# Two early experts instead of the last two hold their gate and up weights outside the ring, and token rows are stored once

## What is computed

```python
x = x + jnp.concatenate([att, lru_out], axis=-1) @ w_out[l]
h2 = rmsnorm(x, ffn_norm[l]).reshape(b * s, d)
# 4 groups of 8 experts; top 1 group, top 2 experts in it; combine = their weights
for g in range(N_GROUPS):
    hg = jax.nn.silu(jnp.einsum('nd,edf->nef', t, w_gate[g])) * jnp.einsum('nd,edf->nef', t, w_up[g])
    y = y + jnp.einsum('nef,efd->nd', hg * combine[:, g, :, None], w_down[g])
x = x + y.reshape(b, s, d)
return rmsnorm(x, final_norm)
```

## Time and profile before

| | us |
|---|---|
| median of 3 runs | 2077.38 |
| lowest, highest | 2074.16, 2081.77 |
| span of the profiled execution | 2074.0 |
| PE busy in it | 1971.6 (95%) |
| third mixture, first to last product of an expert | 1800.7 to 2050.1 |

### The profile page before, as it was taken

The page is one execution under the profiler, slowest core; times in us unless marked ns, Lnnn a source line. Parts: engine busy times, 40 slices in busy tenths (PEclk is TensorE's granted clock), DMA queues, the critical chain, the costliest instruction groups (busy, mean ns, idle before and its releaser), DMA issues.

```text
span 2074.0 us, 25525 instructions
## 1 busy us (share of the span) xinstructions
PE 1971.6 (95%) x10045; PEld 1050.5 (51%) x10045; DVE 691.6 (33%) x1669; ACT 404.9 (20%) x874; POOL 151.7 (7%) x205
## 2 busy tenths in 40 slices
PE   8999889999999999999999999999799999999887
PEld 4444446554545453746554545454554445765443
DVE  0155657311111112635321111112738233632214
ACT  1133433111111111112111111111223322122212
POOL 0111101000000000000100000000010001211100
PEclk9999999999999999999999999999999999999999
DMA  9711104999999999823899999999941111799995
GB/s 334 215 46 47 45 24 166 414 419 420 420 421 420 421 420 378 314 64 102 332 419 420 421 421 420 421 420 417 340 118 41 41 41 33 262 380 419 420 419 216
DMA packets 127026, 596.87 MB, mean 288 GB/s; under 512 B 17489, under 2 KB 46049, under 8 KB 64095
## 3 DMA queue, kind: packets, MB, share of 16 engines
q1 hardware_dynamic: 111567, 568.06, 68.9%
q0 software_dynamic: 15376, 27.68, 4.0%
HBM read 573.48 MB, written 37.01 MB: 294 GB/s over the span
## 4 chain that ended last, share of the span: by engine, by line
PE 81%; DMA 13%; DVE 3%; ACT 2%; issue 1%; SPq 0%; DVEq 0%; ACTq 0%
PE bank L1021 22%; PE bank L679 10%; PE bank L1063 10%; PE bank L930 10%; DMA ring<-in_w_up_dram 7%; DMA ring<-in_moe_w_up_dram 6%; PE bank L826 5%; PE bank L693 4%; PE bank L665 3%; PE bank L1194 1%; PE bank L778 1%; PE bank L755 1%; PE bank L1155 1%; PE bank L921 1%; PE bank L742 1%; PE bank L712 1%
## 5 line engine op out<-in xcount | busy, mean ns | idle before, releaser
L1021 PE MATMUL bank<-ring,work 128*64 128x512 f32 (+1 forms) x2976 | 559.0, 527 | 28.0 <-DMA ring<-in_w_up_dram 24.2
L1021 PEld LDWEIGHTS bank<-ring,work 128*64 128x64 f32 x2976 | 222.7, 138 | 360.2 <-issue 335.5
L1063 PE MATMUL bank<-ring,work 128*64 128x512 f32 x1280 | 295.8, 600 | 3.9 <-DVE work L1894 3.9
L1894 DVE COPY work<-bank 128x256 f32<-128x256 f32 (+1 forms) x96 | 36.5, 380 | 693.8 <-PE bank L922 693.8
L930 PE MATMUL bank<-work 128*128 128x128 f32 x2048 | 245.7, 278 | 0.0
L930 PEld LDWEIGHTS bank<-work 128*128 128x128 f32 x2048 | 233.5, 192 | 6.1 <-issue 2.0
L679 PE MATMUL bank<-hT,ring 128*128 128x512 f32 x512 | 234.2, 599 | 0.7 <-ACT work L1257 0.7
L1353 ACT ACTIVATE work<-bank 64x512 f32<-64x512 f32 x96 | 56.7, 590 | 540.8 <-PE bank L1063 540.8
L1063 PEld LDWEIGHTS bank<-ring,work 128*64 128x64 f32 x1280 | 84.2, 136 | 144.0 <-issue 129.1
L679 PEld LDWEIGHTS bank<-hT,ring 128*128 128x128 f32 x512 | 92.4, 191 | 104.6 <-issue 102.6
L1341 ACT ACTIVATE work<-bank 64x512 f32<-64x512 f32 (+1 forms) x96 | 49.8, 518 | 476.2 <-PE bank L1021 476.2
(11 more groups left out here) (314 smaller groups left out, 1717.8 us busy)
## 6 DMA issues: line engine op xcount, KB each, us to landing
ring<-in_moe_w_down_dram SPq DMA_DIRECT2D x128, 1024.0 KB, 16.3
ring<-in_moe_w_gate_dram SPq DMA_DIRECT2D x126, 1024.0 KB, 15.3
ring<-in_moe_w_up_dram SPq DMA_DIRECT2D x126, 1024.0 KB, 17.3
ring<-in_w_down_dram SPq DMA_DIRECT2D x32, 1024.0 KB, 26.3
ring<-in_w_gate_dram SPq DMA_DIRECT2D x30, 1024.0 KB, 22.1
ring<-in_w_up_dram SPq DMA_DIRECT2D x30, 1024.0 KB, 24.4
ring<-in_attn_w_qkv_dram SPq DMA_DIRECT2D x12, 1024.0 KB, 12.8
work<-y_rows SPq DMA_DIRECT2D x12, 1024.0 KB, 7.0
```

The lines of the kernel that those rows point to most:

```text
L1021: mm = pe.matmul(GU2[s % 2][BLK * a:BLK * a + BLK, 0:F], xgT[pair % 2][:, per * kk + k, BLK * of_pair:BLK * of_pair + BLK], v[a][k], start ...
L1063: mm = pe.matmul(DN[BLK * n:BLK * n + BLK, :], hT_[:, 2 * kk + k, :], v[:, k, 512 * n:512 * n + 512], start=(kk + k == 0), stop=(2 * kk + ...
```

## The change

- The pairs that stay outside the ring in the third mixture are those of experts 2 and 3 counted from 0 (the third and fourth). `load_spare` (expert 2, to `hT`) and `load_scraps` (expert 3, to `work` and the scraps) are called after SP's `slot` 3 instead of after `slot` 2. The scraps have a semaphore of their own. Experts 30 and 31 take their gate and up through the ring. The helpers count the experts of `spare_of` up to a slot instead of counting from the end.
- `x_rows` has 512 rows instead of 1024 and POOL stores each token row once. DVE adds one instruction that halves the row numbers into `x_row`, by which the rows are fetched; POOL's wait for row numbers (`slots_known`) comes after it.
- POOL's load of the final norm's gain waits for two uses of the pairs outside the ring (`spare_used`) instead of one.
- In the second block's mixer the semaphores `par.conv` and `par.forget` become one: DVE, ACT and PE each wait for all ten small loads.

```diff
-        spare_of = [range(E - n, E) for n in (1, 1, 2)]
+        spare_of = [(E - 1,), (E - 1,), (2, 3)]
...
         def spare_slot(m, i, s):
-            return spares_to(m, i, s) > 0
+            return type(i) is int and TURN * i + s in spare_of[m.l]
         def spares_to(m, i, s):
-            return max(0, TURN * i + s - E + 1 + len(spare_of[m.l])) if type(i) is int else 0
+            return sum(x <= (TURN * i + s if type(i) is int else TURN) for x in spare_of[m.l])
         def gu_unit(m, i, s):
-            return 0 if type(i) is int and TURN * i + s == 0 else m.upb * s - m.nd - SPARE * max(0, spares_to(m, i, s) - 1)
+            return 0 if type(i) is int and TURN * i + s == 0 else m.upb * s - m.nd - SPARE * (spares_to(m, i, s) - spare_slot(m, i, s))
...
-                    sources = expert_units(m, l, E - 1)
+                    sources = expert_units(m, l, spare_of[l][0])
...
-                    gate, up, _ = list(expert_units(m, l, E - 2))
+                    gate, up, _ = list(expert_units(m, l, spare_of[l][1]))
...
-                    if l == 2 and type(i) is int and j == 2:
+                    if l == 2 and type(i) is int and j == 3:
                         load_spare()
                         load_scraps()
...
+                    if l == 2:
+                        link(ins)
+                        ins = dve.tensor_scalar(x_row[:, :], y_row[:, :], 1, None, ALU.logical_shift_right)
                     ins.then_inc(slots_known, 1)
...
-                    pool.dma_start(x_rows[2 * P * tt:2 * P * tt + 2 * P, :].rearrange("(p k) d -> p k d", k=2),
-                                   hn[:, tt, :].unsqueeze(1).to_broadcast([P, 2, D])).then_inc(x_stored, 16)
+                    pool.dma_start(x_rows[P * tt:P * tt + P, :], hn[:, tt, :]).then_inc(x_stored, 16)
...
-                        pool.wait_ge(spare_used, 1)
+                        pool.wait_ge(spare_used, 2)
...
-            dve.wait_ge(par.conv, 128)
+            dve.wait_ge(par.conv_forget, 160)
```

More of the change, by code:

```diff
@@ L97, in program @@
     slot_token = [nc.dram_tensor(f"slot_token{l}", (rows_, 1), f32, kind="Internal").ap() for l in range(3)]
-    x_rows = nc.dram_tensor("x_rows", (2 * S, D), f32, kind="Internal").ap()
+    x_rows = nc.dram_tensor("x_rows", (S, D), f32, kind="Internal").ap()
     with ExitStack() as c:
@@ L118, in program @@
         ovi = sb("ovi", [P, 32], u32)
-        y_row = sb("y_row", [P, E // 2], u32)
+        y_row, x_row = sb("y_row", [P, E // 2], u32), sb("x_row", [P, E // 2], u32)
         over_in, over_out = sb("over_in", [P, 2 * T], u32), sb("over_out", [P, 2 * T], u32)
@@ L141, in program @@
         last_added = sem("last_added")
-        spare_loaded, spare_used = sem("spare_loaded"), sem("spare_used")
+        spare_loaded, scraps_loaded, spare_used = sem("spare_loaded"), sem("scraps_loaded"), sem("spare_used")
         xg_loaded = [sem(f"xg_loaded{i}") for i in range(2)]
@@ L168, in __init__ @@
                 self.ln, self.pscale, self.rms0 = sem("par_ln"), sem("par_pscale"), sem("par_rms0")
-                self.conv, self.wab, self.forget = sem("par_conv"), sem("par_wab"), sem("par_forget")
+                self.conv_forget, self.wab = sem("par_conv_forget"), sem("par_wab")
                 self.rms12 = sem("par_rms12")
@@ L411, in program @@
                   con[:, C_CAUS:C_CAUS + 256], sm(128, 256)]
-        last_gates = [spare[0].rearrange("p a n -> p (a n)").rearrange("p (k n) -> p k n", k=K)[:, k, :] for k in range(K)]
-        last_ups = [spare[1].rearrange("p a n -> p (a n)").rearrange("p (k n) -> p k n", k=K)[:, k, :] for k in range(K)]
+        hT_gates = [spare[0].rearrange("p a n -> p (a n)").rearrange("p (k n) -> p k n", k=K)[:, k, :] for k in range(K)]
+        hT_ups = [spare[1].rearrange("p a n -> p (a n)").rearrange("p (k n) -> p k n", k=K)[:, k, :] for k in range(K)]
         spare_up = lnp.rearrange("p (k n) -> p k n", k=K)
@@ L527, in load_scraps @@
                 def load_scraps():
-                    gate, up, _ = list(expert_units(m, l, E - 2))
+                    gate, up, _ = list(expert_units(m, l, spare_of[l][1]))
                     sp.wait_ge(tiles_written, turns[HEADS[l][1]].src_all)
-                    sp.dma_start(spare_up, up).then_inc(spare_loaded, 16)
+                    sp.dma_start(spare_up, up).then_inc(scraps_loaded, 16)
                     sp.wait_ge(routing.ranks, T * (l + 1))
@@ L534, in load_scraps @@
                     for k in range(K):
-                        sp.dma_start(scraps[k], gate[:, k, :]).then_inc(spare_loaded, 16)
+                        sp.dma_start(scraps[k], gate[:, k, :]).then_inc(scraps_loaded, 16)
                 def load(i, v, src):
@@ L1009, in gate_up @@
                                 v = [[spare[a][:, k, :] for k in range(per)] for a in range(2)]
-                            elif last_slot(i, s):
-                                v = [last_gates, last_ups]
+                            elif spares_to(m, i, s) == 1:
+                                pe.wait_ge(spare_loaded, 16 * SPARE * (l + 1))
+                                v = [hT_gates, hT_ups]
                             else:
-                                pe.wait_ge(spare_loaded, 16 * SPARE * (l + 1) + 16 * (K + 1))
+                                pe.wait_ge(scraps_loaded, 16 * (K + 1))
                                 v = [scraps, [spare_up[:, k, :] for k in range(K)]]
@@ L1109, in bank_of @@
                 return bank[r % 8]
-            pe.wait_ge(par.forget, 32)
+            pe.wait_ge(par.conv_forget, 160)
             bk = bank_of(R_F)
@@ L1403, in _ @@
             act.wait_ge(b2.f, 1)
-            act.wait_ge(par.forget, 32)
+            act.wait_ge(par.conv_forget, 160)
             copy_result(fb[0], R_F, ACT.Identity, 8, bias=bfg)
@@ L2224, in _ @@
             for i in range(4):
[L2225 to L2229, removed]
+                vector(taps[:, i, :], t["conv_w_2"][0, i:i + 1, :], par.conv_forget)
+            vector(convp[:, 16:20], t["conv_b_2"], par.conv_forget)
+            vector(convp[:, 20:24], t["b_a_2"].rearrange("l n i -> l (n i)"), par.conv_forget)
+            vector(convp[:, 24:28], t["b_x_2"].rearrange("l n i -> l (n i)"), par.conv_forget)
+            vector(convp[:, 28:32], t["lru_lambda_2"], par.conv_forget)
             pool.dma_start(wf, t["w_in_2"][0][:, 1536:1544].rearrange("(k p) n -> p k n", p=P))\
-                .then_inc(par.forget, 16)
+                .then_inc(par.conv_forget, 16)
             pool.dma_start(bfg, t["b_forget_2"].rearrange("a n -> n a"), allow_slow_non_contiguous=True)\
-                .then_inc(par.forget, 16)
+                .then_inc(par.conv_forget, 16)
             for a, n in enumerate(("w_a_2", "w_x_2")):
```

4 lines of the change are left out of this document (2 added, 2 removed).

## The result

The change makes the kernel a little slower. Over 20 runs of each the median goes from 2079.40 to 2083.89 us; the ratio is 1.0023 with a 95% interval of 1.0014 to 1.0033, that is 4.8 us (2.9 to 6.9) against the forecast of 2.6.

What follows compares the result with a forecast made beforehand. The prediction took full DMA engines in the third mixture, with PE waiting 24.2 us for up weights, as the bound. -2.0 + 16.2 + 1.2 + 0.1 - 12.9 = +2.6 on 2077.4 gave 2080.0 us, range 2072.5 to 2087.

Steps and rivals of the forecast that it cites:

- the lead: Head of the third mixture: four units fewer issued by 1842 let later loads land 2.0 us sooner (0 to 2.7).
- six units and the gain: Stream's end, up of 29 to up of 31: six units take 16.2 us, the final norm's 0.5 MB load adds 1.2.
- from landing to PE's start: At expert 31: 0.1 us between the landing of its up unit and the start of its gate and up.
- PE's pace of before: Kernel before: gate and up of 31 follow the landing of 29's up unit by 12.9 us, two experts' work; subtracted.
- Early in the mixture the engines aren't full: Third mixture: DMA share 0.32 before the loads outside the ring, 0.59 at 1828 to 1832; loads wait for ring units.
- The small backlog: Engines' work in hand, read at 1838.36: down of expert 6 took 7.7 us against 5.0 alone, so 2.7 us.
- a rate under 400 GB/s at the end: Sign in the profile after, at the stream's end: it would show the pace of 2.7 us a unit to be wrong.
- The tail behind expert 31: After gate and up of 31: same work, pair 14's store possibly late for tile 0; taken as 0, upper end 2 us.
- The costs at nothing: Experts 2 and 3 in time, rows stored once, halved row numbers (at most 0.2 us), joined wait (uncovered up to 2): 0.
- A: Rival, chance 0.12: the stream makes up the lost time; gate and up of 31 start 6.1 us sooner, 2071.3.
- B: Rival, chance 0.08: PE's clock falls after a wait at the last expert, costing up to 6 us more, 2086.
- C: Rival, chance 0.10: early loads do not slip; before and after differ by less than 1 us, 2077.

Runs made afterwards that it cites:

- the gain late: Changed kernel with the final norm's gain loaded after the store of pair 14 instead of pair 13: 1.0016 of before, 241.8 us to expert 31.
- the tail cut by columns: Changed kernel with gate and up of experts 30 and 31 loaded to an eighth of their columns on 128 partitions: 0.9995 of before.
- the rest of the change only: Kernel before with rows stored once, row numbers halved and semaphores joined, experts 31 and 30 still outside the ring: 1.0003 of before.
- 2.75 MB less at the head: Kernel before with its three large loads outside the ring cut to an eighth, by columns (0.9986 of before) or to 16 partitions (1.0003).
- experts 25 and 26: Changed kernel with experts 25 and 26 outside the ring, issued where the kernel before issued its own pair: 0.9968 of before.
- 27 and 28: Changed kernel with experts 27 and 28 outside the ring: 0.9967 of before, 234.4 us to expert 31.

## Why the prediction was right, point by point

**The direction and the mechanism held.** The forecast was 2080.0 against 2077.4, +2.6 us; measured are +4.8 (2.9 to 6.9) by the ratio and +3.8 in the two profiles. The mean of the two profiles with 2 and 3 and the gain early (243.5, 243.3) stands 3.2 us over that of the two with the last pair (239.7, 240.7). So the change is 0.23%, within the 0.5% that the prediction took for what a measurement of this kernel can tell; 20 runs of each do better than that and tell it from none. The median itself came out 3.9 us over the forecast, and 2.0 us of these are the kernel before, whose median went from 2077.38 over 3 runs to 2079.40 over 20.

The sum with its terms as the two profiles have them, beside -2.0 + 16.2 + 1.2 + 0.1 - 12.9 = +2.6: the lead -0.65, six units and the gain +17.13, from landing to PE's start +0.13, PE's pace of before -12.85, together +3.76. Two terms were off in opposite directions, the lead by 1.35 and the tail by 0.3.

**One reading of the trace was too broad.** "Early in the mixture the engines aren't full" rests on 0.32 and 0.59. The first lies ahead of the mixture, and the 0.59 is the only such window from 1796 to 1852: the 13 others stand at 0.97 to 1.05, the 0.98 shown above among them. The engines of the kernel before have little slack at the head; it is in the changed kernel, without the four megabytes, that they idle (0.57, 0.56, 0.80 and 0.21 from 1832 to 1848). The small backlog, on which the lead rests, was read from the landings and held.

**The lead of 2.0 us is the term that was too large.** In the two profiles gate and up of expert 29 gain 0.6 us (227.0 to 226.4); over the like kernels it is 227.5 against 226.2, 1.3 us. I had taken the shortest landing, 5.0 us, for the first load after the gap, and 2.5 us more for the next. The down unit of expert 6, issued into nearly idle engines, took 7.1 and the gate of 8 behind it 5.9 us; landing in the changed kernel, issued at 1846.2 and 1849.8:

```profile
DMA to landing us min/median/max: 7.1/7.1/7.1
...
DMA to landing us min/median/max: 5.9/5.9/5.9
```

The same down unit, at the same place of the same order, took 4.9 us in the profile with the gain late and 6.3 in that with the tail cut by columns, so 7.1 is in part this execution's; what makes it differ no run here settles. Counted from expert 0, the up unit of expert 8 landed 1.1 us sooner than before, that of expert 10 1.7 and that of expert 29 0.65. PE's first wait moved an expert later, as forecast: expert 13 no longer waits, where it waited 0.41 us before, and 14 comes 0.35 us behind PE's pace (the first wait that the profile marks is that of 15, 2.82 us). The uncertainty of one profile is about 1 us.

**The pace at the end held, though the rate fell.** Six units and the gain took 17.1 us from product to product; the sum had 16.2 + 1.2 = 17.4. Without the gain 15.8, or 2.64 us a unit where I took 2.70. The gain's own price was 1.3 for 1.2. The prediction had named a rate under 400 GB/s at the end as the sign that its pace was wrong. The sign came (354 and 264 GB/s from 2044 to 2052, behind 424 at 2036 to 2040) and the pace held all the same. So the mean rate of the last few microseconds does not give the pace of the landings. The prediction put that down to the slowest engines; no view here parts the 16 engines, and it stays an inference. The Trainium skill, DMA: Bandwidth & Descriptors, section Specifications, gives about 358 GB/s to a core, from which the prediction's estimate of 2.93 us a unit was worked out; the traces do not agree with it, they have 2.64 to 2.75.

**The tail behind expert 31 held at 0.** The store of pair 14 was issued 0.15 us ahead of the gate and up of 31, where it had been 2.2 us behind, and landed in 5.6 us instead of 2.6: 2.3 us sooner issued (the prediction had 1) and 3.0 longer on its way. DVE of the changed kernel, tile 0 and what follows it:

```profile
2062.41 2.61 DVE L1477 SCALAR_TENSOR_TENSOR h<-work,h 128x1024 f32<-128x1024 f32 x2 [3.23 <-DMA work<-y_rows]
2065.15 1.41 DVE L1503 TENSOR_TENSOR h<-h,bank 128x512 f32<-128x512 f32 x2
```

The wait grew from 2.57 to 3.23 us and the 0.8 us in hand before L1503 (of before: L1502) shrank to 0.1. It cost nothing, with almost nothing left over. The high end of the sum also holds a 0.4 of which the prediction names only 0.2, the halved row numbers; neither shows in the time of the rest of the change.

**The costs at nothing held.** There was no wait on `hT` or a scrap: gate and up of experts 2 and 3 start 16.9 and 28.0 us after those of expert 0, as before. The joined wait moved DVE's wait from 8.97 to 9.40 us, and it still idles over 22 us later:

```profile
1518.88 0.16 DVE L2001 SCALAR_TENSOR_TENSOR small<-small 128x4 f32<-128x4 f32 x1 [9.40 <-DMA small<-in_b_forget_dram]
...
1556.76 0.68 DVE L2021 SCALAR_TENSOR_TENSOR work<-work 8x512 f32<-8x512 f32 x1 [22.84 <-ACT work L1394]
```

The kernel with the rest of the change only (1.0003) shows rows and join together at no cost that can be measured, within 2.7 us below and 3.7 above.

**The rivals.** A, the stream that catches up, is out for this change: the share of 0.21 was not made good, and 2.75 MB less at the head moved nothing by 7 us. But its figure, gate and up of 31 some 6 us sooner, is nearly what experts 25 and 26 reach (5.2 us sooner, 234.5 where 233.5 was worked out), where no unit is missing at the head: the arithmetic was near and its condition wasn't met. B, the slow clock at the last expert, did not happen in the changed kernel's profile and did in that of 25 and 26, for 1.8 us. In the starved stretch the same fall costs nothing: of before, the product of expert 15 took 5.36 us, and that of expert 16, 8.1 us later, started without a wait. C, no move at all, is out: the interval excludes 1.

## What to carry to other kernels

A buffer beside the ring is worth what the stream does while it is filled and while it is used. Fill it while the transfer engines would idle, and use it late, but far enough from the end that the consumer has worked through at its own pace when the last transfer lands: here, with 25 and 26 or 27 and 28, that gave 0.3%, with 2 and 3 it cost 0.2%. Count how many units have been issued at the moment at which two versions of an order become equal again. If the stream is full from there on, the difference is paid at its end, at 2.6 to 2.7 us a unit here, and only the engines' backlog at that moment comes off it.

## What was not expected of the hardware

- A load of 128 KB onto 16 partitions, four of them in a full stream, took the whole stream from 418 to 424 GB/s down to 252 to 305 at a share of 0.98 to 1.03. The same bytes over 128 partitions in rows of 1 KB did not delay it: expert 29 came at 226.2 us as in the changed kernel. The two ways of cutting differ in the length of a row as well (8 KB and 1 KB), and no run parts that from the number of partitions.
- The moments of two executions (the kernel before, and it with the rest of the change) are alike to 0.1 us for 88 us of the mixture and then part by 1 us with the same order of weight loads (227.0 and 228.0 to expert 29), so that a lead of 0.6 us in one pair of profiles is not a measurement of it.
